# Attention's steps interleaved with the z and u products, and the adaptive modulation sums regrouped, in a two-layer single-core kernel

## The reference

```python
c_act = silu(c)
for layer in (0, 1):
    shift, scale, gate = split(c_act @ ada_w[layer, 0] + ada_b[layer, 0], 3)
    h = rmsnorm(x) * (1 + scale) + shift
    if layer == 0:      # even mixer
        q, k, v, u, z = split(h @ mix_w_in, 5)              # 512 features each
        o_a = dilated_attention(q, k, v)                    # 8 heads of 64
        zn = rmsnorm(gelu(z)) * norm_g
        mixed = einsum('gij,bcjgd->bcigd', tril(sgu_w), zn) + sgu_b
        y = concat([o_a, gelu(u) * mixed]) @ mix_w_out
    else:               # RWKV7 time mix: r, k, v products, small products for
        y = rwkv7(h)    # decay, a and g, then a chunked recurrence
    x = x + gate * y
    shift, scale, gate = split(c_act @ ada_w[layer, 1] + ada_b[layer, 1], 3)
    h = rmsnorm(x) * (1 + scale) + shift
    x = x + gate * moe(h)   # router picks 2 of 16 experts for each token
out = rmsnorm(x) * final_norm_g
```

## Time and profile before

| | us |
|---|---|
| median of 3 runs | 1554.78 |
| lowest and highest | 1553.16, 1559.13 |
| the profiled execution | 1548.98 |
| its span | 1547.0 |

### The profile page before, as it was taken

One profiled execution on the slowest core, in us unless ns is written; L12 is line 12 of the kernel. 1 busy time (PEld: TensorE's weight loads), 2 busy tenths in 40 slices (PEclk: granted clock), 3 DMA queues, 4 the chain that ended last, 5 costly groups with the idle time before them and its releaser, 6 DMA issues.

```text
span 1547.0 us, 23213 instructions
## 1 busy us (share of the span) xinstructions
PE 1336.6 (86%) x8816; PEld 811.9 (52%) x8816; DVE 671.6 (43%) x1373; ACT 357.6 (23%) x806; POOL 254.8 (16%) x263
## 2 busy tenths in 40 slices
PE   0899979997799994699999799999999895999990
PEld 0444557756344441343443688888887454444440
DVE  6426434564133233805026556666763324232324
ACT  1100035102111111101048433333332102211111
POOL 1000037000010012100001423444431200100102
PEclk9999867897899997799999899999997997899995
DMA  8649655373599995311110000000001313699975
GB/s 312 205 143 353 205 191 191 129 252 118 183 348 372 355 355 207 127 55 55 55 54 1 29 3 3 19 2 3 3 2 48 116 55 123 206 344 350 372 274 203
DMA packets 128997, 248.35 MB, mean 161 GB/s; under 512 B 8352, under 2 KB 78192, under 8 KB 128912
## 3 DMA queue, kind: packets, MB, share of 16 engines
q1 hardware_dynamic: 116816, 203.09, 37.9%
q0 software_dynamic: 7344, 26.74, 4.7%
q10 hardware_dynamic: 4752, 17.30, 2.7%
HBM read 219.33 MB, written 27.79 MB: 160 GB/s over the span
## 4 chain that ended last, share of the span: by engine, by line
PE 81%; DVE 8%; issue 4%; DMA 3%; ACT 2%; POOL 1%; POOLq 0%; DVEq 0%; SPq 0%; ACTq 0%
PE PS L1905 15%; PE PS L1723 11%; PE PS L1715 9%; PE PS L1922 7%; PE PS L1767 7%; PE PS L2049 2%; PE PS L2065 2%; PE PS L1894 2%; PE PS L2019 2%; PE PS L2071 2%; PE PS L1698 2%; PE PS L1954 2%; DMA arena<-in_ada_w 2%; PE PS L2104 1%; PE PS L1839 1%
## 5 line engine op out<-in xcount | busy, mean ns | idle before, releaser
L1905 PE MATMUL PS<-WR,arena 128*128 (+1 forms) x528 | 238.8, 606 | 11.3 <-ACT arena L1036 6.2
L1723 PE MATMUL PS<-arena,WR 128*128 128x512 f32 x384 | 168.0, 597 | 3.4 <-ACT arena L970 3.4
L1905 PEld LDWEIGHTS PS<-WR,arena 128*128 128x128 f32 x528 | 99.7, 194 | 128.5 <-issue 124.3
L1715 PE MATMUL PS<-WR,arena 128*128 128x512 f32 x320 | 143.1, 607 | 3.8 <-DVE arena L1478 3.8
L1723 PEld LDWEIGHTS PS<-arena,WR 128*128 128x128 f32 x384 | 73.3, 192 | 96.4 <-issue 92.8
L1922 PE MATMUL PS<-W,arena 128*128 x264 | 119.0, 593 | 3.9 <-DVE arena L1412 3.9
L1207 DVE SCALAR_TENSOR_TENSOR arena<-arena,cact 128x1024 f32<-128x1024 f32 x77 | 98.8, 1283 | 36.5 <-DMA arena<-in_ada_w 31.8
L1767 PE MATMUL PS<-WR,arena 128*128 128x512 f32 x256 | 112.2, 595 | 0.0
L1401 DVE TENSOR_TENSOR arena<-arena,PS 128x256 f32<-128x256 f32 x33 | 13.9, 421 | 212.1 <-ACT arena L1049 191.1
L1715 PEld LDWEIGHTS PS<-WR,arena 128*128 128x128 f32 x320 | 61.6, 195 | 83.2 <-issue 76.3
L796 POOL TENSOR_TENSOR LO<-GB,tmp 128x256 f32<-128x256 f32 x80 | 71.0, 906 | 100.6 <-DVE GB L1540 72.6
(11 more groups left out here) (321 smaller groups left out, 2062.3 us busy)
## 6 DMA issues: line engine op xcount, KB each, us to landing
WR<-in_moe_w SPq DMA_DIRECT2D x66, 1024.0 KB, 7.5
arena<-in_ada_w SPq DMA_DIRECT2D x96, 512.0 KB, 5.2
W<-in_moe_w SPq DMA_DIRECT2D x33, 1024.0 KB
expert_rows<-arena ACTq DMA_DIRECT2D x33, 512.0 KB, 7.2
WR<-in_rwkv_w_rkv SPq DMA_DIRECT2D x6, 2048.0 KB, 7.9
WR<-in_mix_w_in SPq DMA_DIRECT2D x5, 2048.0 KB, 10.6
WR<-in_mix_w_out SPq DMA_DIRECT2D x2, 2048.0 KB, 8.1
expert_rows<-arena SPq DMA_DIRECT2D x1, 4096.0 KB, 14.3
```

The source lines that it names most:

```text
L1715: last = mm(out, act_T[:, c, b * P:(b + 1) * P], WR[:, tile % 2, c, :], start=(c == 0), stop=(c == KC - 1))
L1723: last = mm(out, WR[:, tile % 2, c, f * P:(f + 1) * P], act_T[:, c, :], start=(c == 0), stop=(c == KC - 1))
L1905: last = mm(PS[:, 2, :], XgT[:, c, :], WR[:, slot, c, :].rearrange("p s f -> p (s f)"), start=(c == 0), stop=(c == KC - 1))
```

## The change

- The loop's z and u products: TensorE's order was v, u, mod(2), z, loop. Now it is v, mod(2), and inside the loop every even step n below 16 begins with one product of eight matmuls, of z for n = 0 to 6 and of u for n = 8 to 14. ScalarE does the Gelu (and z's square) at the start of the same steps, ahead of the exponentials. The swT transposes go from ahead of the loop to step 8 (`SWT_AT`), and the mix work moves from step 4 to step 10 (`MIX_AT`).
- Attention's and the gating's transposed outputs go to areas of their own, `OT0` and `ST0`, since HT is still read by the products. Steps 16 and 17 also hold gate(0) (step 16) and the first two output products (`out_unit`); gate(0)'s diagonal is made at step 15 on VectorE.
- Sums: three instead of two behind each q drain, four instead of three for each k, one for each v; none between v and the loop; in the loop one in steps 0 to 7 and two in steps 8 to 15, behind the step's scores. GpSimd's eight sums become VectorE's.
- The 24 sums of L = 3, which layer 1's router needs, leave `residual(0)` and go, with mod(4), into the second layer: loads behind tile(8) and `x_done` 16, sums ahead of the mixes of m = 2, TensorE's mod(4) between gl and r1, VectorE's behind the mixes of m = 4.
- SP: the spare rows are filled from X, early. tile(3) (now z's weights) comes behind all loads of L = 1; tile(4) (u), 5 and 6 among those of L = 2.

```diff
+SWT_AT, MIX_AT = 8, 10
...
     for n in range(NPAIR + 3):
+        if n < NPAIR and n % 2 == 0:
+            add("z" if n < NPAIR // 2 else "u")
+        if n == SWT_AT:
+            add("swT")
+            add("swT")
         if n < NPAIR:
             add("score")
             add("score")
-        if NB <= n < 2 * NB:
+        if 0 <= n - MIX_AT < NB:
             add("mix")
         if n >= 2 and n - 2 < NPAIR:
             add("pT")
             add("pT")
         if n >= 3 and (n - 3) % PPB == 0:
             add("o", "b")
-        if NB + 2 <= n < 2 * NB + 2:
+        if 0 <= n - MIX_AT - 2 < NB:
             add("sT")
         if n >= 3 and (n - 3) % PPB == PPB - 1:
             if n == NPAIR + 2:
                 add("mod")
             add("oT")
+        if n == NPAIR:
+            add("gate")
+            add("gate")
+        if NPAIR <= n < NPAIR + 2:
+            add("y")
...
+        OT0 = LO[:, 0:2048].rearrange("p (b c t) -> p b c t", b=NB, c=4)
+        ST0 = arena[:, 5, 0:2048].rearrange("p (b c t) -> p b c t", b=NB, c=4)
...
-        tiles = [(io["mix_w_in"][0], n * 512) for n in range(5)] + [(io["mix_w_out"][0], n * 512) for n in range(2)]
-        tile_last = [("q", 3), ("k", 3), ("v", 3), ("u", 3), ("z", 3), ("y", 3), ("y", 7)]
+        tiles = [(io["mix_w_in"][0], n * 512) for n in (0, 1, 2, 4, 3)] + [(io["mix_w_out"][0], n * 512) for n in range(2)]
+        tile_last = [("q", 3), ("k", 3), ("v", 3), ("z", 3), ("u", 3), ("y", 3), ("y", 7)]
...
+            for k in (NEXP, NEXP + NB):
+                sp.dma_start(y_dram[k * P:(k + NB) * P, :].rearrange("(b p) f -> p b f", p=P), X
+                             ).then_inc(sem("rest_out"), 16)
...
             for m in range(3 * KC):
                 ada(1, m)
-                if m % 8 == 3:
-                    tile(2 + m // 8)
+                if m == 3:
+                    tile(2)
+            tile(3)
             for m in range(4):
                 ada(2, m)
+            tile(4)
+            for m in range(4, 10):
+                ada(2, m)
             tile(5)
-            for m in range(4, 12):
+            for m in range(10, 3 * KC):
                 ada(2, m)
             tile(6)
-            for m in range(12, 3 * KC):
-                ada(2, m)
-            sp.wait_ge(*free("u", 4))
-            sp.wait_ge(*free("k", 4))
-            sp.wait_ge(*free("q", 4))
-            sp.wait_ge(*free("v", 4))
-            sp.dma_start(y_dram[NEXP * P:MAX_ITEMS * P, :].rearrange("(k p) f -> p k f", p=P),
-                         arena[:, 3:5, :].rearrange("p a (k f) -> p (a k) f", f=D)).then_inc(sem("rest_out"), 16)
-            for m in range(3 * KC):
-                ada(3, m)
...
+            sp.wait_ge(sem("x_done"), 16)
+            for m in range(3 * KC):
+                ada(3, m)
...
+            def gelu(n):
+
+                if n < NPAIR // 2:
+                    b = n // 2
+                    act.wait_ge(*full("z", b + 1))
+                    nc.scalar.activation(Z0[:, b, :], bank("z", b), ACT.Gelu).then_inc(drained["z"], 1)
+                    act.wait_ge(*free("z", b + 1))
+                    nc.scalar.activation(GB[:, 0:WA], Z0[:, b, :], ACT.Square, accum_out=ss[:, b:b + 1]
+                                         ).then_inc(sem("zss_ready"), 1)
+                else:
+                    b = n // 2 - NB
+                    act.wait_ge(*full("u", b + 1))
+                    nc.scalar.activation(U0[:, b, :], bank("u", b), ACT.Gelu).then_inc(drained["u"], 1)
+
             for n in range(NPAIR + 3):
+                if n < NPAIR and n % 2 == 0:
+                    gelu(n)
+                if n == SWT_AT:
+                    for k in range(2):
+                        act.wait_ge(*full("swT", k + 1))
+                        nc.scalar.copy(SWT[:, 4 * k:4 * k + 4, :], bank("swT", k).rearrange("p (c t) -> p c t", c=4)
+                                       ).then_inc(drained["swT"], 1)
                 if n < NPAIR:
...
-                some_ada(2)
+                some_ada(3)
             mod(1)
             for f in range(4):
-                some_ada(3)
+                some_ada(4)
                 v.wait_ge(*full("k", f + 1))
             for b in range(NB):
                 v.wait_ge(*full("v", b + 1))
                 nc.vector.tensor_copy(V0[:, b, :], bank("v", b)).then_inc(drained["v"], 1)
-                some_ada(3)
+                some_ada(1)
             mod(2)
-            some_ada(12)
-
-            rms(1, sem("zss_ready"), 4, WA)
-            v.wait_ge(sem("gz_in"), 16)
 
             for n in range(NPAIR + 3):
-                if NB < n <= 2 * NB:
-                    b = n - NB - 1
+                if n == MIX_AT - 2:
+                    rms(1, sem("zss_ready"), 4, WA)
+                    v.wait_ge(sem("gz_in"), 16)
+                if n == NPAIR - 1:
+                    diag(0, 0)
+                if 0 <= n - MIX_AT - 1 < NB:
+                    b = n - MIX_AT - 1
...
-                if n < NB:
-                    stt(Z0[:, n, :], Z0[:, n, :], rstd[:, n:n + 1], gz, ALU.mult, ALU.mult).then_inc(sem("zn"), 1)
-                    some_ada(1)
-                elif NB < n <= 2 * NB:
+                if 0 <= n - MIX_AT + 2 < NB:
+                    k = n - MIX_AT + 2
+                    stt(Z0[:, k, :], Z0[:, k, :], rstd[:, k:k + 1], gz, ALU.mult, ALU.mult).then_inc(sem("zn"), 1)
+                if n < NPAIR:
+                    some_ada(1 if n < NPAIR // 2 else 2)
+                if 0 <= n - MIX_AT - 1 < NB:
...
-            del todo[0:8]
-            diag(0, 0)
             mod(3)
-            some_ada(8)
             router_weights(0)
-            residual(0, lambda n: some_ada(4 if n < 4 else 0))
+            residual(0)
...
+                    if m == 2:
+                        some_ada(3 * KC)
+                    if m == 5:
+                        mod(4)
...
-            for n, kind in enumerate(("v", "u", "z")):
-                tile_ready(pe, 2 + n)
-                for b in range(NB):
-                    rows(kind, b, b, 2 + n, HT)
-                if kind == "u":
-                    mod(2)
+            tile_ready(pe, 2)
+            for b in range(NB):
+                rows("v", b, b, 2, HT)
+            mod(2)
             pe.wait_ge(*free("q", 4))
             pe.wait_ge(*free("k", 4))
-            pe.wait_ge(*free("v", 4))
-            pe.wait_ge(sem("consts"), 10)
-            for k in range(2):
-                out = open_bank(pe, "swT", k)
-                for c in range(4):
-                    last = nc.tensor.transpose(out[:, c * P:(c + 1) * P], SW[:, 4 * k + c, :], ident[:, :])
-                last.then_inc(filled["swT"], 1)
             for n in range(NPAIR + 3):
+                if n < NPAIR and n % 2 == 0:
+                    kind, b = ("z", n // 2) if n < NPAIR // 2 else ("u", n // 2 - NB)
+                    if b == 0:
+                        tile_ready(pe, 3 if kind == "z" else 4)
+                    rows(kind, b, b, 3 if kind == "z" else 4, HT)
+                if n == SWT_AT:
+                    pe.wait_ge(sem("consts"), 10)
+                    for k in range(2):
+                        out = open_bank(pe, "swT", k)
+                        for c in range(4):
+                            last = nc.tensor.transpose(out[:, c * P:(c + 1) * P], SW[:, 4 * k + c, :], ident[:, :])
+                        last.then_inc(filled["swT"], 1)
+                if n == 3:
+                    pe.wait_ge(*free("v", 4))
                 if n < NPAIR:
                     i, pair = n // PPB, n % PPB
-                    if n == 0:
-                        pe.wait_ge(sem("zss_ready"), 4)
                     outs = [open_bank(pe, "score", 2 * n + hh) for hh in range(2)]
                     for hh in range(2):
                         lo = HD * hh
                         mm(outs[hh][:, 0:(i + 1) * P], qT[lo:lo + HD, pair, i * P:(i + 1) * P],
                            kT[lo:lo + HD, pair, 0:(i + 1) * P], start=True, stop=True).then_inc(filled["score"], 1)
-                if NB <= n < 2 * NB:
-                    b = n - NB
+                if 0 <= n - MIX_AT < NB:
+                    b = n - MIX_AT
...
+                if NPAIR <= n < NPAIR + 2:
+                    b = n - NPAIR
+                    if b == 0:
+                        gate(0)
+                        tile_ready(pe, 5)
+                        pe.wait_ge(*free("sT", 4))
+                    pe.wait_ge(*free("oT", b + 1))
+                    out_unit(0, 5, 0, b)
             pe.wait_ge(*free("oT", 4))
-            pe.wait_ge(*free("sT", 4))
-            out_proj(0, 5)
+            out_proj(0, 5, 2)
...
-                if layer == 0:
-                    mod(4)
...
                 small("gl", 1, open_bank(pe, "gl", 1)[0:32, :], G1L[:, :, P:P + 32], XM[1], 3)
+                mod(4)
                 pe.wait_ge(sem("mixed"), 40)
```

102 lines of the change are left out of this document (36 added, 66 removed).

## The result

The changed kernel takes **1562.5 us** (median of 5 runs, 1558.1 to 1565.8), the kernel before beside it 1556.0 (5 runs, 1553.2 to 1559.1). The ratio on record is 1.0068, with a 95% interval of 1.0037 to 1.0099: slower, by 5.8 to 15.4 us. Predicted were 1558.7 us and +3.9, with a range that holds the time; the rise is larger than forecast and, by the ratio on record, falls into the case "slower by over 0.5%", to which I had given 0.26. The profiled execution took 1558.08 us, span 1556.3, against 1548.98 and 1547.0 before.

A forecast was written before the change was run, and what follows sets the result against it. TensorE, carrying 81% of the chain of work, was taken to bound the kernel. First layer -6.4, mod(4) +10.4 and -0.1 gave +3.9 us: 1552.9 profiled, 1558.7 us on the timed runs' scale, range 1544 to 1570.

The forecast's parts named there:

- +10.4: Second layer: mod(4) between the gl and r1 products, 8.0 us plus 2.4 us lost to half clock in r1.
- -6.4: First layer: sum of the changes from v's start to the third output product, in us.
- start of v: v's first product waits for the drain of q's last bank, behind a third sum: +1.8 us.
- gap before z: z waits for the sums of L=1, mod(2)'s last third and its weights, starting at 151.5: +5.4 us.
- loop: z, u and attention interleaved: 51 us work, 11.7 waits and 3.4 clock against 79.6 before: -13.5 us.
- gate(0), mod(3) with oT: First layer behind attention: gate(0) -1.6 us at better clock, mod(3) with oT -1.2 us by beginning at full clock.
- after it: Between oT and the third output product: wait for y0's bank on VectorE and a low-clock tail, +2.7 us.
- two such dips of about 1.7 us: Interleaved loop: TensorE's granted clock falls twice behind pauses, 3.4 us in all.
- Rival 2: Loop, steps 2 to 9: clock falls in each gap, four more slow products, about +10 on the forecast, 1568.5 us; chance 0.17.
- Rival 1: Loop: ScalarE and VectorE keep ahead, clock stays 1.00, some 3 us of waits; -8 us, 1546.5 us; chance 0.23.
- Rival 3: Loop: a table switch costs twice its row, three waits grow 1.28 us each, +3.8, 1562.5 us; chance 0.05.
- Rival 4: Second layer: sums of L=3 end at 705, al, gl and r1 products wait, +4 to +8, 1564 us; chance 0.05.

The follow-up runs named there:

- experiment 1: Changed kernel with mod(4) and the sums of L=3 put back beside the first router; ratio 1.0009 to the kernel before, span 1544.2 us.
- experiment 2: Kernel before with only mod(4), the sums of L=3 and their loads moved to the second layer; ratio 1.0064, span 1557.9 us.
- experiment 8: Kernel before with seven unused products of 0.88 us ahead of the scores in step 3 of attention's loop; ratio 0.9962, profiled span 1550.0 us.
- experiment 9: Kernel before with seven unused products in step 3, plus two more ahead of the scores in each of steps 3 to 9; ratio 0.9975.
- experiment 10: Kernel before with seven unused products in step 3, plus one more ahead of the scores in each of steps 3 to 9; ratio 0.9947.
- experiment 5: Changed kernel with Gelu of z and u replaced by a copy, read up to the router only; 136.27 us from z's first product to mod(3).
- experiment 6: Changed kernel with mod(2) in step 3 ahead of the first pv and tile(3) queued behind load (1, 11); ratio 1.0110 to the kernel before.
- experiment 3: Changed kernel with VectorE's modulation sums moved behind the softmax division OB in each step; ratio 1.0048 to the kernel before, span 1559.7 us.

## Why the prediction came out as it did

The forecast of +3.9 us was a sum of +10.4, -6.4 and -0.1. The first term measured 10.34 in the trace and is confirmed from both sides (experiments 1 and 2). The second measured 0: **that term failed**, by its clock. That the time lies in the range is owed to the range, 26 us wide, and not to this term; the case with the largest chance, within 0.5% of no change (0.52), is not the one that came by the ratio on record.

| first layer | predicted | measured | from |
|---|---|---|---|
| start of v | +1.8 | +1.0 | 109.66 - 108.66; counted from mod(1)'s start (106.18 and 106.96) it is +1.8 |
| v itself | 0 | +1.6 | 29.24 up to mod(2) instead of 27.6: low clock behind the 1.64 us wait |
| gap before z | +5.4 | +3.3 | 146.05 and 150.31: 2.57 + 0.69 idle |
| loop | -13.5 | -7.1 | 72.5 us of loop instead of 79.6 |
| gate(0), mod(3) with oT | -2.8 | -2.6 | 1.84; 9.14 up to the end of oT |
| after it | +2.7 | +3.4 | 7.28 from oT's end to lbias |

The loop's 72.5 us are z's first product to mod(3), 145.70, less the eight products (55.2), the 2.4 of the low clock in the first, gate(0) (1.84) and two output products (13.8). Against the forecast 66.1 (51 work + 11.7 waits, whose six terms add up to 11.8, + 3.4 clock) the waits are 2.14 + 1.60 + 2.01 + 1.88 + 2.76 = 10.4, near what was said; the clock is 1.75 each in two z products, 3.9 in step 11, 1.1 in the product behind it and 1.6 in step 15: **10.1**; 52.0 is left as work. So the mis-sized term is "I count two such dips of about 1.7 us, 3.4": two came at that price, and three more pieces ran at the half clock, in whole or in part. I had taken the 2.54 us pause of the earlier trace rows as about the least that costs the clock. The runs show pauses of 1.6 to 2.8 us costing it at most places (here not at 199.93, behind 2.01), and 0.72 us or less not costing it ahead of a dense product, where the clock was up before. The same holds at v, behind 1.64 us, for which nothing was forecast. With 10.1 and 1.6 in its place the sum is -6.4 + 6.7 + 1.6 = +1.9; the gap, 2.1 less than forecast, brings it back to about 0, and that the two cancel is luck. (The measured column adds up to -0.4; the rest is a few tenths of mod(2) and of the product behind it.)

The reading of the kernel before was incomplete too. I said that the half clock of 213 to 247 us "follows a pause of 6.5 us". It does, but in experiment 8 the pause is gone and the profiled execution has the half clock all the same, while the clocks of its timed runs suggest that about half of them didn't have it. Experiments 9 and 10 leave the steps as they are and put one or two wide products between them, and it stays up each time. The rows allow a sum of what the interleaving gained in the loop. Before, the 79.6 us were 51 of work, 12.4 idle and 16.3 lost to the half clock; after, the 72.5 are 52.0, 10.4 and 10.1. So 2.0 us came from waits and 6.2 from the clock: by this sum most of the gain is that the wide products stand between small steps, and not the time of the overlap. No experiment separates the two.

- Rival 2, the clock in the gaps, is what happened, at two thirds of its price: +6.7 in the loop against its +10, and 1.6 in v, where it had none. It came closest in mechanism, and I gave it 0.17 with the row beside it in which small waits of 0.9 us kept 0.99, which is true and doesn't reach to 2 us.
- Rival 1, the overlap hides more, failed: of the six waits that were listed five came, 10.4 us; of the 0.8 us in step 9 there is 0.1.
- Rival 3, the table switch at twice its row: refuted, 1.40 us.
- Rival 4, late sums of L=3: no wait of TensorE before mod(4), in the changed kernel or in experiment 2; the sums ended at 693.9 in the changed kernel, where 697.4 was forecast.
- The gap's forecast rested on z's weights landing at 151.5 and on sums ending at 147.8; z started at 150.31. Right in kind, 1 us early.
- "A granted clock near 1 from z's second product to mod(3)" was the sign that failed; the late third of mod(2), the Exp loads, the OB waits, mod(4)'s 7.9 us and r1's slow head came as written, and v's start at 109.66 instead of 110.4. None of the three signs of being wrong came (z by 147, waits under 4 or over 18, r1 within 3 us of gl's end): they watched the waits, and the term that failed was the clock.

## What to carry to other kernels

Where TensorE works in steps of small products, ask of each pause, even one of 2 us, what clock the work behind it will have: here the clock cost as much as the waits themselves (10.1 and 10.4 us). Before a rewrite that interleaves engines, try the cheap form first: unused wide products in the long pause and one in each step gave 0.5% here, and in the pause alone 0.4%, where the interleaving gave nothing. And a block of work is free only in its place: mod(4) cost nothing while the router waited, and 10.3 us between dense products.

## What the runs showed of the hardware

- A table load between two activations cost 1.40 us from instruction to instruction (1.28 in its own row), with no idle time on either side.
- In the profiled execution of experiment 8, TensorE, busy 26.91 of 27 us, stayed at 1.2 GHz throughout while its pieces were small (64 to 256 columns), and in that of experiment 10 it was at 2.4 GHz with the same pieces and one product of 512 columns in each step. The Trainium skill (TensorE: Matmul & The Clock Gate, "A second HAM failure mode: psum-queue depth-cycling") tells of a bf16 kernel with 512 columns in which short idle moments between groups of matmuls bring the clock down again and again. The changed kernel agrees in kind from step 3 on (8.78 instead of 7.09 us behind waits of 2.14 and 1.60); the stretch of experiment 8, low though it has hardly any idle time, isn't covered by it.
- The same pause doesn't cost the same each time. Behind a 1.88 us wait, the mix of step 11 took 3.67 us in the changed kernel and 2.00 in experiments 1, 5 and 6. Behind a 2.01 us wait, the product of step 8 took 7.08 us in the changed kernel, 8.02 in experiment 1 and 7.97 in experiment 5. The product behind the 1.60 us wait in step 5 took 8.78 us in all four executions that have this wait unfilled (the changed kernel, experiments 1, 3 and 6).
- mod's products of one column are followed by low clock although TensorE is busy in them: the 8.05 us of mod(3) in the changed kernel were granted 0.65, and the 7.28 us from oT's end to lbias 0.53.
